# Moving output-projection steps, bank assignments and two small stages between loop turns of three attention stages, in a four-layer transformer kernel on one Trainium2 core

## The reference, cut to what matters

```python
for layer in range(DEPTH):                       # first block, DEPTH = 2
    h = rmsnorm(x, attn_norm[layer])
    # layer 0: 8 "fox" heads and 8 "dsa" heads; layer 1: 16 "moba" heads
    x = x + concat(heads) @ w_out                # 256x1024 @ 1024x1024
    x = x + conv_glu_ffn(rmsnorm(x, ffn_norm[layer]), w_up, conv_w, conv_b, w_down)
...
attn_out = _mla_attention(q_nope, q_rope, k_nope, k_rope, v)       # second block, 8 heads
hm = _mlstm_chunkwise(mq, mk, mv, ig, fg)                          # 4 heads
hm = (hm - mean(hm)) * rsqrt(var(hm) + EPS) * mh_norm_g
ml_out = (hm + ml_skip * xc) * silu(z)
x = x + concat([attn_out, ml_out]) @ w_o
x = x + _hier_moe(rmsnorm(x), ...)
```

## Time and profile before

| | |
|---|---|
| median of 3 runs | 1070.53 us (1070.38 to 1070.63) |
| the profiled execution's own time | 1070.63 us |
| its span in the trace | 1068.8 us |
| PE busy | 1021.6 us (96%) |
| DVE busy, ACT busy, POOL busy | 630.5, 534.3, 86.5 us |
| granted PE clock, mean | 0.99 |

### The profile page before, as it was taken

How to read it: one execution, slowest core, us unless ns; L and a number is a source line. 1 busy time by engine, 2 the same in 40 slices (tenths; PEclk the granted TensorE clock), 3 DMA queues, 4 the chain that set the end, 5 groups by cost and what they waited for, 6 DMA issues and landing times.

```text
span 1068.8 us, 15373 instructions
## 1 busy us (share of the span) xinstructions
PE 1021.6 (96%) x6023; PEld 785.0 (73%) x6023; DVE 630.5 (59%) x1242; ACT 534.3 (50%) x941; POOL 86.5 (8%) x98
## 2 busy tenths in 40 slices
PE   6999899999999999999999999997979999999977
PEld 5776599999888876799999888775755454545435
DVE  4777678888646566678888547668642121212156
ACT  6667665555536456565555437756522121212155
POOL 0100002112000211001211002100000000000000
PEclk9999999999999999999999999999989999999999
DMA  8824255654655433356565563154549999999931
GB/s 278 308 95 142 80 158 161 195 197 160 200 194 192 161 119 119 118 160 195 160 197 198 181 188 116 54 164 172 183 140 411 409 409 409 409 409 409 405 114 40
DMA packets 112672, 224.62 MB, mean 210 GB/s; under 512 B 10559, under 2 KB 65234, under 8 KB 112594
## 3 DMA queue, kind: packets, MB, share of 16 engines
q1 hardware_dynamic: 112434, 223.04, 59.2%
q10 hardware_dynamic: 160, 0.53, 0.1%
HBM read 222.50 MB, written 1.05 MB: 209 GB/s over the span
## 4 chain that ended last, share of the span: by engine, by line
PE 87%; DVE 7%; ACT 3%; issue 1%; SPq 1%; DMA 1%; DVEq 0%; ACTq 0%
PE ps L543 83%; PE ps L547 4%; DVE wl L1872 1%; DVE smb L1886 1%; SPq L2777 1%; DMA ring<-in_w_in_even_dram 1%; DVE xs L1872 1%; ACT hh L1336 0%; DVE smb L1872 0%; ACT wh L1339 0%; ACT xh L1339 0%; SPq L2774 0%; DVE pb L1877 0%; DVE hl L1882 0%; ACT xg L1336 0%
## 5 line engine op out<-in xcount | busy, mean ns | idle before, releaser
L1872 DVE TENSOR_TENSOR wl<-ring,wh 128x1024 fp32r<-128x1024 f32 (+3 forms) x212 | 278.6, 1323 | 131.9 <-ACT wh L1339 130.7
L1339 ACT ACTIVATE wh<-ring 128x1024 fp32r<-128x1024 f32 (+3 forms) x212 | 222.6, 1052 | 147.7 <-PE ps L543 143.3
L543 PE MATMUL ps<-hh,wh 128*128 128x256 f32 x768 | 219.2, 286 | 1.4 <-DVE sA L1872 1.0
L543 PE MATMUL ps<-hh,wl 128*128 128x256 f32 x768 | 217.2, 284 | 0.0
L543 PE MATMUL ps<-hl,wh 128*128 128x256 f32 x768 | 215.5, 284 | 0.0
L543 PEld LDWEIGHTS ps<-hh,wh 128*128 128x128 f32 x768 | 147.9, 193 | 3.2 <-issue 1.4
L543 PEld LDWEIGHTS ps<-hh,wl 128*128 128x128 f32 x768 | 147.9, 193 | 0.0
L543 PEld LDWEIGHTS ps<-hl,wh 128*128 128x128 f32 x768 | 146.9, 193 | 0.3
L543 PE MATMUL ps<-ring,xg 128*64 128x512 f32 x320 | 85.5, 595 | 0.0
L543 PE MATMUL ps<-wh,hh 128*128 128x512 f32 (+3 forms) x192 | 79.3, 413 | 3.6 <-DVE wl L1872 3.5
L2725 POOL TENSOR_TENSOR fs<-fs,rt 128x256 f32<-128x256 f32 x44 | 52.5, 1212 | 368.3 <-ACT fs L1336 368.3
(11 more groups left out here) (287 smaller groups left out, 1691.7 us busy)
## 6 DMA issues: line engine op xcount, KB each, us to landing
ring<-in_w_up_dram SPq DMA_DIRECT2D x88, 512.0 KB, 4.7
ring<-in_w_down_dram SPq DMA_DIRECT2D x22, 1024.0 KB, 5.0
ring<-in_w_gate_e_dram SPq DMA_DIRECT2D x40, 512.0 KB, 7.7
ring<-in_w_up_e_dram SPq DMA_DIRECT2D x40, 512.0 KB, 9.0
ringx<-in_w_down_e_dram SPq DMA_DIRECT2D x16, 1024.0 KB, 8.4
ring<-in_w_down_e_dram SPq DMA_DIRECT2D x16, 1024.0 KB, 9.8
ring<-in_w_in_odd_dram SPq DMA_DIRECT2D x12, 1024.0 KB, 5.1
ringx<-in_w_gate_e_dram SPq DMA_DIRECT2D x24, 512.0 KB, 9.8
```

The source lines that it names most:

```text
L543: return e.matmul(o, l, r, start=start, stop=stop)
L1339: return e.activation(o, i, ACT.Copy)
L1872: return e.tensor_tensor(o, a, b, op)
```

## The change

Five things are edited, and no arithmetic.

1. Stage 1: steps 5 to 8 of the output projection move from turns 12, 13, 15, 16 to turns 11, 12, 13, 14 on PE and ACT. DVE, which had put off what belongs to turn 9 until after turn 11, now takes each split one turn after the other engines throughout.
2. Layer 1: banks 0, 1 and banks 2, 3 change places in the output projection, in `ffn(1)` and its norm, so that layer 1 has the numbers that layer 0's feed-forward part has. The projection's banks become (0, 1, 2, 3), the default.
3. Stage 2, ACT: `mix_hi("moba0", 1)` moves from the end of turn 12 to the end of turn 13.
4. Stage 3, PE: a step of the projection comes before the `value` of the same turn and no longer after it.
5. Stage 3, DVE: the first four pieces of `hm_steps`, which ran at turns 11, 11, 12 and 13, run at the end of turns 11, 12, 13 and 14, behind the turn's split.

The hunks stand in the order of the file: common lists; PE in layer 1, in stage 2 and in stage 3; ACT in stage 2; DVE in stage 1 and in stage 3.

```diff
-        out_at = ((8, 8, 9, 10, 12, 13, 15, 16, 18, 19, 20), range(13, 21), range(11, 15))
+        out_at = ((8, 8, 9, 10, 11, 12, 13, 14, 18, 19, 20), range(13, 21), range(11, 15))
...
-            norm_banks = {"fn0": (4, 5, 0, 1), "an1": (6, 7, 2, 3), "fn1": (4, 5, 2, 3), "nm2": (6, 7, 2, 3)}
+            norm_banks = {"fn0": (4, 5, 0, 1), "an1": (6, 7, 2, 3), "fn1": (4, 5, 0, 1), "nm2": (6, 7, 2, 3)}
...
-                    row_scale(claim((0, 2)[l], "rb", f"fn{l}"), f"fn{l}", l + 1)
+                    row_scale(claim(0, "rb", f"fn{l}"), f"fn{l}", l + 1)
...
-                            (((2, 3, 6, 7), (0, 1, 4, 5)), ((0, 1, 6, 7), (2, 3, 4, 5)))[l][s % 2], lambda: next(side, None), s == 0)
+                            (0, 1, 4, 5) if s % 2 else (2, 3, 6, 7), lambda: next(side, None), s == 0)
...
-                         ((0, 1, 4, 5), (2, 3, 4, 5))[l])
+                         (0, 1, 4, 5))
...
-                             mixed("moba0", "moba1"), (2, 3, 0, 1), mixed_high(4))
+                             mixed("moba0", "moba1"), high=mixed_high(4))
...
+                if i in out_at[2]:
+                    next(outp)
                 if i >= 3:
                     n, h = order2[i - 3]
...
-                if i in out_at[2]:
-                    next(outp)
...
-                if i in (11, 12):
-                    mix_hi("moba0", i - 11, bank_of(mh2, i - 11))
+                if i in (11, 13):
+                    mix_hi("moba0", (i - 11) // 2, bank_of(mh2, (i - 11) // 2))
...
-                for _ in range(out_at[0].count(i - 1) if i != 10 else 0):
+                for _ in range(out_at[0].count(i - 1)):
                     next(outp)
-                if i == 11:
-                    for _ in range(out_at[0].count(9)):
-                        next(outp)
...
                 if i == 11:
-                    next(hms)
-                    next(hms)
                     next(proj)
-                if i in (12, 13):
-                    next(hms)
...
                 if i - 1 in out_at[2]:
                     next(outp)
+                if 11 <= i < 15:
+                    next(hms)
```

## The result

| | before | after |
|---|---|---|
| median, first measurement (4 executions each) | 1070.45 us | 1080.13 us |
| lowest to highest | 1069.39 to 1070.63 | 1078.59 to 1081.10 |
| the profiled execution, its span | 1070.63, 1068.8 us | 1081.88, 1080.1 us |
| granted PE clock, mean | 0.99 | 0.98 |

The ratio is 1.0094, 95% interval 1.0081 to 1.0107; the medians lie 9.7 us apart, where 5.4 was forecast and 1079.6 was the range's upper end. Measured again later beside 24 executions of before, the same kernel stood at 1.0062 (1.0042 to 1.0082), +6.7 us. After's own median hardly moved between the two (1080.13 and 1080.60), before's did (1070.45 and 1073.89).

What follows compares the result with a forecast made beforehand. PE, busy for 96% of the span, was taken as the bound. The terms 5.2 + 1.8 - 1.3 - 0.3 = +5.4 us on the profiled execution's 1070.6 gave 1076.0 us, range 1073.0 to 1079.6.

Steps and rivals of the forecast that it cites:

- part 2: Stage 2, first projection step: PE waits for bank 1 because `mix_hi` now stands behind turn 13's split, 5.2 us.
- Part 1: Layer 1: the renumbered banks cost 0 in `ffn(1)`, hidden in waits that exist anyway.
- part 3: Stage 2, behind the stall: one or two stretches of low PE clock cost 1.8 us, bounds 0.8 and 2.4.
- Part 4: Stage 1: PE waits of 3.65 us replace 4.97 of gaps and low clock, -1.3 us, bounds -1.7 and +0.4.
- Part 5: Stage 3: PE idles 4.3 us before the second projection step, the 3.11 shrinks; -0.3 us, bounds -1.9 and +1.0.
- the rule of the Trainium skill: Stage 3: POOL reading SBUF blocks two-SBUF-input DVE instructions, never reductions; about 1.0 of the subtraction's 3.31 us goes.
- What PE loses or gains before that point moves everything behind it: Before the experts: until the full ring stops transfers at 766 to 768, PE's delays or gains shift everything later.
- the rival without a stall: Stage 2: bank 1 drained by 424, so no stall or slow clock; 1069.0 us, or 1067.1; chance 0.10.

Runs made afterwards that it cites:

- shift3: The kernel before with 30 extra matmuls (3.6 us) in the fourth step of `ffn(1)`: ratio 1.0033 (1.0018 to 1.0048), +3.5 us.
- shift7: The kernel before with 60 extra matmuls (7.2 us) in the fourth step of `ffn(1)`: ratio 1.0057 (1.0037 to 1.0077), +6.1 us.
- banks_only: The kernel before with only the bank numbers of layer 1 changed, `mix_hi` left at turn 12: 1075.92 us, ratio 1.0026 (1.0006 to 1.0045).

## Why the prediction was wrong

**Direction and mechanism: right.** One idle gap inside the first projection step of stage 2, released by DVE `ml`, with `mix_hi` behind the split of turn 13, as written. The stall of 5.2 (part 2) measured 5.25, 5.24 and 5.2 in three traces. Part 1, banks in layer 1 at no cost elsewhere: right, `ffn(1)` took 189.0 us with either numbering.

**The step that failed: the clock behind that stall (part 3).** It was taken as 1.8 us with 2.4 as the upper bound, from two places where the low stretch was 3.4 and 6.8 us long. It measured 3.7 to 4.1 in three traces: the stretch was 13.6 us, it began near the start of the stall (0.2 us into it in two of the traces, 1 us ahead of it in after), and some 8 us of full PE work ran in it once PE resumed. The bound was drawn from the longest stretch seen, and nothing in the rows excluded a longer one. The step also ordered the gaps by their length, with 1.40 us as the longest that kept the clock. Length alone doesn't order them: the trace of before has a gap of 2.38 us that kept 1.00 (1035.83, shown above), and elsewhere the clock fell behind gaps of 0.67 and 0.62 us.

**Part 4, stage 1, -1.3: the figure was met, the reason was not.** The idle gaps came where they were said to (1.50 before the transposes of head 8, 1.36 before those of head 14) and the sum of idle time moved little, 3.54 before and 3.31 after (22.46 us less 19.15 busy), where 3.65 was worked out. But the term was all made of a low stretch that would not come; it comes or stays away in either order. At equal clock the edit gives 0.0 in stage 1, and in three of the four traces with edit 1 and stage 2 unedited the low stretch stood in stage 2, for 1.5 us.

**Part 5, stage 3, -0.3:** measured -0.7 to -2.6 in seven traces, mean -1.3, inside the bounds but for one of the seven. The gap before the second step was 4.10 (4.3 forecast), the wait for `mla_lo` shrank from 3.11 to 0.46. DVE and POOL in after, answering to the earlier trace rows:

```profile
742.18 1.22 DVE L1894 TENSOR_REDUCE st<-xs 128x8 f32<-128x1024 f32 x1
743.43 1.40 DVE L1877 TENSOR_SCALAR st<-st 128x8 f32<-128x8 f32 x1
744.87 1.23 DVE L1872 TENSOR_TENSOR xs<-xs,st 128x1024 f32<-128x1024 f32 x1
748.05 1.22 DVE L1872 TENSOR_TENSOR wl<-ring,wh 128x1024 fp32r<-128x1024 f32 x1 [1.96 <-ACT wh L1339]
```

```profile
742.44 2.37 POOL L2744 TENSOR_TENSOR sA<-sA 128x1024 f32<-128x1024 f32 x1 [54.04 <-ACT sA L1336]
```

The subtraction fell from 3.31 to 1.23, since POOL had ended at 744.81; the reduction beside POOL kept its 1.22. In its place the tiny scaling of 128x8 took 1.40 and ended with POOL; it took 1.40 or 1.41 in all seven traces with edit 5 and 0.17 in before. So the rule of the Trainium skill (SBUF — State Buffer, "Who interferes with whom") holds in both halves, the reduction being free included; the rest of that section, that a scaling can take the shared port too, was not weighed, and took back 1.2 of the 2.1 us that the subtraction gained. The chain gained about 0.9 us.

**The way to the end.** "What PE loses or gains before that point moves everything behind it": true of delays (shift3, shift7). Missing was that the last gate product costs 0 or 1.2 to 4.3 more from execution to execution, in this kernel and in others alike, and that the profiled execution of before was one that paid nothing. The sum was made against a cheap execution. Besides, the lower end of the rival without a stall is a slip: -1.3 and -1.9 give 1067.4 and not 1067.1, which moves no chance.

**The account.** In the traces stage 2 is 5.2 + 3.9 = +9.1 (9.0 to 9.3), stage 1 nothing, stage 3 about -1.3: +7.8. The larger measurement gave +6.7 (4.5 to 8.8). The first one gave +9.7, with four executions of before as low as the lowest sixth of the later ones; its interval, 8.7 to 11.5, leaves +7.8 out, and why those four were so low is open. The forecast, +5.4, is 2.4 short of +7.8: 2.1 at the clock and 1.3 at stage 1, less 1.0 that stage 3 gave beyond its term. How often each stretch comes with either kernel was not settled; 17 traces are too few.

## What to carry to other kernels

A stall in a stretch where PE is otherwise full costs its own length and, in the five traces here, some 4 us of half clock, for stalls from 1.5 to 5.2 us alike: price it by the length of work at half clock, not by the stall, and don't bound it by the longest stretch in one trace. Before a term is taken from a low stretch that an edit would remove, get a second trace of the unchanged kernel: stretches near gaps of 0.6 to 2.5 us come and go by 0 to 4 us each, and four executions taken together all lay at one end. When a copy drains a bank that the next step on PE claims, keep it ahead of whatever else its engine does in that turn.

## What was not expected of the hardware

- At 1.2 GHz stretches of 3.4, 6.8, 10.2 and 13.6 us were seen, the longest with a stall of 5.2 us, 10.2 us with one of 1.5 us; in banks_only and after the fall came ahead of the stall, behind gaps of 0.67 and 0.62 us.
- Identical code, 0.15 us apart in the span, ran at either clock: 16 transposes in 1.97 or 3.68 us behind gaps of 2.38 and 2.28 us.
- 22 dummy matmuls in a stall shortened the low stretch from 13.6 to 3.4 us; 19 in two gaps of 2.4 and 2.3 us kept the clock at 1.00 behind them in three traces of three, where it had fallen in the 14 without them.
- A DVE scaling of 128x8 took 1.40 us beside POOL's product of SBUF tiles, a reduction of 128x1024 beside it its usual 1.22; without POOL the scaling took 0.17.
- In three kernels with 19, 24 and 30 matmuls more a new gap of 1.5 to 2.1 us stood inside the last transposes, in four with 15, 22, 34 and 60 more none did; the cause is open.
